# A two-layer hybrid decoder step on one core: GpSimd rounds some weight tiles, the gates become tangents, the convolution starts later, and other keepers

## The reference, cut to what matters

```python
def _mixer(h, st, pos, lb, p):
    ...
    proj = (h @ p['w_in']).astype(f32)
    ...
    conv = xcat[:, :T] * p['gdn_conv_w'][0]
    for j in range(1, GDN_CONV):
        conv = conv + xcat[:, j:j + T] * p['gdn_conv_w'][j]
    conv = jax.nn.silu(conv)
    ...
    gates = jax.nn.sigmoid(proj[..., OFF_GATE:])
    merged = None
    for n, y_b in enumerate((y_rw, y_ret, y_gdn, y_hg)):
        term = gates[..., n * D_MODEL:(n + 1) * D_MODEL] * (y_b @ p['w_branch'][n])
        merged = term if merged is None else merged + term
    out = merged.astype(h.dtype) @ p['w_out']
```

## Time and profile before

| | us |
| --- | --- |
| runs shown | 2711.17, 2693.80, 2695.78 |
| median | 2695.78 |
| profiled execution, its own time | 2704.68 |
| its span in the profile | 2702.9 |
| TensorE busy | 2361.5 (87%) |
| Vector busy | 1138.1 (42%) |
| GpSimd busy | 844.8 (31%) |
| ScalarE busy | 731.2 (27%) |

### The profile page before, as it was taken

How to read it: one execution, slowest core, us unless ns; L and a number is a source line. 1 busy time by engine, 2 the same in 40 slices (tenths; PEclk the granted TensorE clock), 3 DMA queues, 4 the chain that set the end, 5 groups by cost and what they waited for, 6 DMA issues and landing times. The chain is left out here.

```text
span 2702.9 us, 46568 instructions
## 1 busy us (share of the span) xinstructions
PE 2361.5 (87%) x20592; PEld 2176.8 (81%) x20592; DVE 1138.1 (42%) x1558; ACT 731.2 (27%) x915; POOL 844.8 (31%) x602
## 2 busy tenths in 40 slices
PE   5878978689899989999977789777898899999997
PEld 3767866578778979999976679656787699999997
DVE  5164464555444532221233546655734445222212
ACT  2432311322212232222224333104222133322222
POOL 2311210133133434444432213101322234444442
PEclk8988988889999999999988989778999999999998
DMA  6331121111232324322233311111112322222222
GB/s 250 118 110 57 60 72 46 45 51 45 80 102 87 117 88 127 120 91 87 94 120 117 105 54 59 61 55 48 52 52 73 115 77 102 79 94 94 87 93 73
DMA packets 68457, 233.39 MB, mean 86 GB/s; under 512 B 10784, under 2 KB 11296, under 8 KB 67872
## 3 DMA queue, kind: packets, MB, share of 16 engines
q1 hardware_dynamic: 61344, 214.88, 24.1%
q10 hardware_dynamic: 6912, 15.53, 1.6%
HBM read 219.03 MB, written 11.35 MB: 85 GB/s over the span
## 5 line engine op out<-in xcount | busy, mean ns | idle before, releaser
L735 POOL TENSOR_TENSOR ring_lo<-ring,w_hi 128x512 fp32r<-128x512 f32 x552 | 769.9, 1416 | 1429.8 <-ACT w_hi L1355 1361.2
L803 PE MATMUL gm<-H_hi,ring_lo 128*128 128x260 f32 x3456 | 749.2, 299 | 98.1 <-ACT GT L1594 34.1
L803 PE MATMUL gm<-H_hi,w_hi 128*128 128x260 f32 x3456 | 720.9, 290 | 0.0
L803 PE MATMUL gm<-H_lo,w_hi 128*128 128x260 f32 x3456 | 719.9, 291 | 0.0
L803 PEld LDWEIGHTS gm<-H_hi,ring_lo 128*128 128x128 f32 x3456 | 559.6, 197 | 142.5 <-ACT GT L1594 39.9
L803 PEld LDWEIGHTS gm<-H_lo,w_hi 128*128 128x128 f32 x3456 | 554.2, 196 | 2.3 <-issue 1.9
L803 PEld LDWEIGHTS gm<-H_hi,w_hi 128*128 128x128 f32 x3456 | 553.7, 195 | 1.6 <-issue 0.8
L1355 ACT ACTIVATE w_hi<-ring 128x1024 fp32r<-128x1024 f32 x268 | 282.9, 1056 | 447.4 <-PE gm L803 186.0
L752 POOL TENSOR_TENSOR X<-X,GT 128x520 f32<-128x520 f32 x32 | 49.8, 1557 | 323.6 <-DVE GT L2277 323.6
L1279 PE MATMUL gm<-AF_hi,ring_lo 128*128 128x260 f32 x704 | 142.1, 283 | 3.3 <-DVE AF_lo L2301 3.3
L1279 PE MATMUL gm<-AF_hi,w_hi 128*128 128x260 f32 x704 | 141.5, 282 | 0.0
(11 more groups left out here) (410 smaller groups left out, 2750.4 us busy)
## 6 DMA issues: line engine op xcount, KB each, us to landing
ring<-wall SPq DMA_DIRECT2D x372, 512.0 KB, 3.3
WB<-wbranch SPq DMA_DIRECT2D x32, 256.0 KB, 3.6
xsave<-X SPq DMA_DIRECT2D x2, 2080.0 KB, 12.1
X<-xsave ACTq DMA_DIRECT2D x8, 520.0 KB, 5.3
arena<-states ACTq DMA_DIRECT2D x8, 512.0 KB, 3.4
sst<-arena ACTq DMA_DIRECT2D x8, 512.0 KB, 3.7
X<-xt SPq DMA_DIRECT2D x1, 2080.0 KB, 12.1
y<-H SPq DMA_DIRECT2D x4, 520.0 KB, 2.7
```

The source lines that it names most:

```text
L735: pool.tensor_tensor(ring_lo[:, SLOT[i], k], ring[:, SLOT[i], k], hi[:, k].bitcast(F32), ALU.subtract).then_inc(parts_ready, 1)
L803: ins = pe.matmul(out[:, hf, 0:HALF], w[a][:, k, :], src[b][:, k, HALF * hf:HALF * (hf + 1)], start=first and a == "lo", stop=last and a == b)
```

## The change

Six things change:

- **GpSimd's tiles.** A set `BUSY` names stages of mixers; a tile whose rounding by ScalarE would fall behind such a stage is in `held_up` and is rounded by GpSimd. By the plan these are 9 tiles in each layer: gated-delta projections 5 and 7, HG's gate 2, RWKV's gates 2, 5 and 7, retention projections 2 and 5, gated delta's gate 2. GpSimd's roundings go from 8 to 26 in all, ScalarE's from 268 to 250.
- **The convolution** yields twice before its first step, so the first two calls of `beside(2)` do less, and the first evacuation of RWKV's scores comes ahead of it.
- **Gates** are tanh(x/2) in place of the sigmoid; Vector's multiply adds 1 first, and the factor 0.5 goes into the copy that rounds the sum `MG` and the subtraction behind it. ScalarE's table loads go from 74 to 64.
- **Keepers in a modulation bank.** `AT_BANK` puts 18, 18 and 12 keepers ahead of the wait for a bank at a modulation task of HG's stage, at RWKV projection 2 and at gated-delta projection 0. They write to the unused second half of a bank with a modulation product.
- **Other counts of keepers**: `AT_START` 14 to 18; `AT_TILE` as in the diff; 8 ahead of HG's samples; at the norm before the FFN 18 and 26 in place of 22. The two at retention's samples and the argument `busy` in RWKV's scores and inverse go; there the bank was closed, and no instruction changes.
- The order of tasks in the plan, the ring and all transfers stay as they are.

```diff
-AT_START, AT_END, AT_FFN_NORM, AT_INNER = 14, 6, 22, 7
-AT_TILE = {("proj", 2, 2): 20, ("proj", 2, 5): 7, ("proj", 3, 1): 15, ("proj", 3, 6): 8, ("gate", 2, 0): 7}
-AT_SAMPLES = {0: (0, 0), 1: (22, 5), 2: (0, 5), 3: (2, 0)}
+AT_START, AT_END, AT_INNER, AT_SUMS, AT_FFN_NORM = 18, 6, 7, (0, 22), (18, 26)
+AT_TILE = {("proj", 2, 2): 8, ("proj", 3, 6): 5, ("gate", 2, 0): 5, ("gate", 1, 7): 5}
+AT_BANK = {("ada", 0, 18): 18, ("proj", 1, 2): 18, ("proj", 2, 0): 12}
+AT_SAMPLES = {0: (8, 0), 1: (22, 5), 2: (0, 5), 3: (0, 0)}
...
+BUSY = {(RW, 3), (RW, 4), (RW, 6), (GD, 0), (GD, 3), (GD, 5), (GD, len(BEFORE[GD])), (GD, len(BEFORE[GD]) + 6), (RT, 0)}
...
-            on_scalar = {j for j, (i, _) in enumerate(splits)
-                         if j >= mixing + 2 and j - mixing - KT not in (0, 1) or (2 <= j < mixing + 2 and room_after[i] <= at[j - 2])}
+            held_up = {j for j in range(3, mixing + 2)
+                       if any(kind == "mix" and (n, m) in BUSY for kind, n, m in plan[at[j - 3]:at[j - 2]])}
+            on_scalar = {j for j, (i, _) in enumerate(splits) if j not in held_up
+                         and (j >= mixing + 2 and j - mixing - KT not in (0, 1)
+                              or (2 <= j < mixing + 2 and room_after[i] <= at[j - 2]))}
...
                 def begin():
                     kind, n, m = tasks[begun[0]]
+                    if (kind, n, m) in AT_BANK and any(half_only):
+                        keep_busy(AT_BANK[kind, n, m], gm[:, half_only.index(True), 1, HALF:HALF + P128])
                     begun[0] += 1
...
-                        act.activation(h2(GT[:, :]), src, ACT.Sigmoid).then_inc(done, 1)
+                        act.activation(h2(GT[:, :]), src, ACT.Tanh, scale=0.5).then_inc(done, 1)
...
                 def convolution():
 
+                    yield
+                    yield
                     from_scalar()
...
-                    step(tt(MG_lo[:, m, :], MG[:, m, :], MG_hi[:, m, :].bitcast(F32), SUB), x_ready)
+                    step(stt(MG_lo[:, m, :], MG[:, m, :], 0.5, MG_hi[:, m, :].bitcast(F32), MUL, SUB), x_ready)
...
-                            taken(tt(h2(GT[:, :]), src, h2(GT[:, :]), MUL), done)
+                            taken(stt(h2(GT[:, :]), h2(GT[:, :]), 1.0, src, ADD, MUL), done)
```

More of the change, by code:

```diff
@@ L759, in _ @@
                 used = [0, 0]
-                bank_open = [False]
+                bank_open, half_only = [False], [False, False]
                 def keep_busy(n, out=None):
@@ L785, in bank @@
                         pe.wait_ge(evac[g % 2], g // 2)
-                    bank_open[0] = True
+                    bank_open[0], half_only[g % 2] = True, False
                     return gm[:, g % 2]
@@ L847, in ada @@
                     out = bank()
+                    half_only[(used[1] - 1) % 2] = True
                     for k in range(0, KT // 2, 2):
@@ L986, in diagonal_scores, with inverse @@
                     return ins
-                def inverse(cp, busy=0):
+                def inverse(cp):
                     def blocks():
@@ L994, in blocks @@
                                 yield u, u // 2 * NC + 2 * cp + u % 2, slice(a, a + BLK), slice(a + BLK, a + 2 * BLK)
-                    operands(FILL_SHORT, busy=busy)
+                    operands(FILL_SHORT)
                     for u, m, i, j in blocks():
@@ L1144, in rwkv @@
                         yield
-                        operands(busy=4 if cp else 21)
+                        operands()
                         scores(0, cp, pj(RW, 1), WK[:, 0])
@@ L1148, in rwkv @@
                         yield
-                        yield from inverse(cp, 4 if cp else 0)
+                        yield from inverse(cp)
                         for ci in range(2):
@@ L1256, in _ @@
                 coming(-1)
-                if layer + 1 == DEPTH:
-                    keep_busy(AT_FFN_NORM, mx[:, 3, 0:P128])
+                keep_busy(AT_SUMS[layer], mx[:, 3, 0:P128])
                 pe.wait_ge(operands_v, count.next(operands_v))
                 feature_sums()
-                keep_busy(AT_FFN_NORM, mx[:, 3, 0:P128])
+                keep_busy(AT_FFN_NORM[layer], mx[:, 3, 0:P128])
                 for m in range(2 * FT):
@@ L1593, in _ @@
                         gates += 1
-                        act.activation(h2(GT[:, :]), src, ACT.Sigmoid).then_inc(done, 1)
+                        act.activation(h2(GT[:, :]), src, ACT.Tanh, scale=0.5).then_inc(done, 1)
                         g[0] += 1
                         if n == RT and m:
-                            step(act.activation(MG_hi[:, m - 1, :], MG[:, m - 1, :], ACT.Copy), for_vector)
+                            step(act.activation(MG_hi[:, m - 1, :], MG[:, m - 1, :], ACT.Copy, scale=0.5), for_vector)
                     if x in rounds_after and rounds_after[x]:
@@ L1600, in _ @@
                 act.wait_ge(gate_used, gates)
-                step(act.activation(MG_hi[:, KT - 1, :], MG[:, KT - 1, :], ACT.Copy), for_vector)
+                step(act.activation(MG_hi[:, KT - 1, :], MG[:, KT - 1, :], ACT.Copy, scale=0.5), for_vector)
                 for k in range(0, KT, 2):
@@ L2273, in _ @@
                             dve.wait_ge(x_saved, 16)
-                            taken(tt(h2(MG[:, m, :]), src, h2(GT[:, :]), MUL), done)
+                            taken(stt(h2(MG[:, m, :]), h2(GT[:, :]), 1.0, src, ADD, MUL), done)
                             step(dve.tensor_copy(NA[:, :], NA[:, :]), gate_used)
                         else:
-                            taken(tt(h2(GT[:, :]), src, h2(GT[:, :]), MUL), done)
+                            taken(stt(h2(GT[:, :]), h2(GT[:, :]), 1.0, src, ADD, MUL), done)
                             if n == RT:
```

## The result

The changed kernel takes 2686.2 us (median of 8 runs, 2670.4 to 2690.2) against 2702.1 for the kernel before (8 runs, the three shown above among them). The ratio of the two, over all runs, is 0.9932, with a 95% interval from 0.9908 to 0.9956. That is 18.4 us faster (6.5 either way; the two medians are 15.9 apart), where 23.5 were forecast. The profiled execution took 2683.4, 21.3 less than that of before.

A forecast was written before the change was run, and what follows sets the result against it. TensorE was taken to bound the mixing stage, with about 130 us of gaps and slower products after them. Terms 12.6 + 4.8 + 4.0 + 2.0 + 1.8 + 1.3 − 3 = 23.5 off 2695.8 gave 2672.3 us, range 2654 to 2695.

The forecast's parts named there:

- a: RWKV's first scores: evacuating them ahead of Vector's convolution wait gains 6.3 us a layer, 12.6 in all.
- given back: Rival, chance 0.12: Vector meets the convolution's steps later with TensorE behind it, so its gain is 0; 2685 us.
- b: GpSimd rounds nine tiles a layer: gated-delta projection 5 starts without waiting, 2.4 us a layer, 4.8 in all.
- g: GpSimd's eighteen extra roundings slow some Vector operations beside them: 3 us lost, ends 0 and 18.
- c: Keepers ahead of the bank wait at gated-delta projection 0: faster large products, 2.0 us a layer, 4.0 in all.
- d: Keepers ahead of the bank wait at RWKV projection 2: 1.0 us a layer, 2.0 in all.
- e: Eight keepers ahead of HGRN2's samples: layer 1's four products take 1.98 instead of 3.78 us, gaining 1.8.
- f: Gates as tangents: fewer table loads, less one new load and a wider Vector multiply; net gain 1.3 us.
- h: Other keeper changes, including those removed at gated-delta projection 2, stand in waits others end; taken at nothing.
- More than the sum: Rival, chance 0.18: TensorE enters RWKV's inverse at a higher clock, 10 us more gained, 2662.3 us.
- Keepers don't hold the clock: Rival, chance 0.20: the keeper gains at both banks and the samples fall away, 7.8 us; 2680 us.
- Slower: Rival, chance 0.06: GpSimd's rounding delays each of 18 tiles and slows two Vector operations; 48 us more, 2744.

The follow-up runs named there:

- run 2: Changed kernel with ScalarE rounding all 18 tiles again instead of GpSimd: 2686.9 us, ratio to the kernel before 0.9930.
- run 3: Changed kernel with sigmoid gates and Vector's plain multiply again: 2677.4 us, ratio to the kernel before 0.9911.
- run 11: Changed kernel with 20 in place of 8 keepers at gated-delta projection 2: 2672.9 us, ratio to the kernel before 0.9884.
- runs 9 to 12: Changed kernel again, 2684.2 us; with sigmoid gates, 2675.8; with 20 instead of 8 keepers at gated-delta projection 2, 2672.9; with both, 2669.7.
- run 7: Kernel before with all the new tables of keepers and nothing else: ratio to the kernel before 0.9990.
- run 4: Changed kernel with all tables of keepers as before: 2687.1 us, ratio to the kernel before 0.9936.
- run 9: Changed kernel measured and traced once more, nothing altered: 2684.2 us, ratio to the kernel before 0.9922.
- kernels 5 and 8: Kernel before with the later convolution alone, ratio to before 0.9938, and with the tangent gates alone, 0.9965.

## Why the prediction was right or wrong, point by point

The time lay in the range and 5 us from the forecast, within 1% of before, as was likeliest. The terms:

- **a, the convolution: mechanism right, the place measured.** Vector gains 6.3 us from the copy to the second evacuation, as worked out. TensorE gains more, 8.3 and 7.7 by the modulation product behind, since it does not go down in clock (1.16 for the 16 scores instead of 2.08); 3.2 and 2.1 of it (the two traces of the changed kernel) go in the next segment of layer 0, in the first at the clock of 0.66. Alone it brings 16.8 us, undone in the changed kernel 5.7. The forecast's 12.6 lies between. The rival "given back" has a part in it, about 3 us of layer 0 in the trace, but not the whole; how much is lost further on is not shown.
- **b, GpSimd's tiles: right at the place.** Projection 5 starts at its bank's release; without GpSimd it waits 3.47. With the part alone, projections 5 and 6 are 2.1 us shorter in each layer, where the term had 2.4. Over the whole kernel alone and undone differ: alone the part brings 6.5 us, where b and g together had 1.8, and undone in the changed kernel it costs nothing (run 2). At RWKV's gate 7 the forecast said that nothing shows because Vector covers it. GpSimd's timeline there:

```profile
589.90 1.61 POOL L757 TENSOR_TENSOR X<-X,GT 128x520 f32<-128x520 f32 x1 [7.93 <-DVE GT L2287]
591.47 2.21 POOL L737 TENSOR_TENSOR w_hi<-ring,CN 128x1024 fp32r<-128x1024 f32 x1
593.76 2.76 POOL L740 TENSOR_TENSOR ring_lo<-ring,w_hi 128x512 fp32r<-128x512 f32 x2
```

and TensorE's, which answers to the earlier trace rows:

```profile
592.55 1.38 PE L772 MATMUL gm<-CN 128*128 128x128 f32 x10 [0.35 <-ACT GT L1602]
595.35 0.80 PE L808 MATMUL gm<-H_hi,ring_lo 128*128 128x260 f32 x2 [1.41 <-POOL ring_lo L740]
```

  The product ends 4.0 us later than before relative to the gate ahead of it, but by retention projection 1 only 1.0 us is left of it in layer 0 and 1.1 in layer 1. So the cover took three quarters.
- **c: right in layer 0.** 2.5 us for gated-delta 0 and 1, and 3.62 for the thirty steps. In layer 1 the segment is 0 to 1.6 us shorter, and the thirty steps take 5.0 to 5.1 in five of the nine traces with the keepers.
- **d: not in the changed kernel's first trace, but in most of the others.** There the products at RWKV projection 2 are still slow behind the keepers, which leave 3.04 us of the wait bare, and the segment from the modulation product ahead of them to RWKV projection 3 changes by -0.5 and +1.2. In the eight other traces with these keepers that segment takes 23.5 to 23.7 us in fourteen layers of sixteen, and in the five with the old ones 24.6 to 25.4: some 1 us, as forecast. TensorE's timeline in the first trace:

```profile
141.07 0.56 PE L808 MATMUL gm<-H_hi,ring_lo 128*128 128x260 f32 x2 [3.04 <-DVE MT L2230]
141.42 0.64 PE L808 MATMUL gm<-H_lo,w_hi 128*128 128x260 f32 x2
```

- **e: right at the place,** 3.78 to 1.98 in layer 1. Over all traces the first of these products is slow in four layers of ten without the keepers and in none of eighteen with them. Beyond the place no run tells it alone.
- **f: the trace has the signs, the runs don't add up.** The loads went and came where they were said to. RWKV's gates 0 to 6 are 2 us a layer shorter with tangents, where the term had 2.6 (over all traces 0.6 to 4.8 shorter than before with tangents, from 1.9 shorter to 2.0 longer with sigmoids); the load in front of the convolution's sigmoid costs 1.1 to 1.4 by the segment up to it (run 3 against the changed kernel), where the term had 1.3. The tangents alone are 9.5 us faster than before, but in the changed kernel three pairs say 5 to 7 us slower. The term +1.3 lies between; segments whose loads are off the path move by more than the loads do, at one place with the clock (0.66 against 0.83). By the Trainium skill (ScalarE: Activation LUTs, section What ACT_TABLE_LOAD costs) a switch is 2.66 us with its drain. The drain doesn't show here: in the earlier trace rows the gate starts at once behind its load, and in the changed kernel two loads off the path bring some 2 us in a layer, which 1.28 each allow and which is less than one such switch.
- **g: right in size as busy time.** Forecast 3 us; Vector is busy 3.6 us more with the tiles on GpSimd, 0 to 5 over all traces. How much of it is on the path isn't shown. The one case that is shown on the path is not of these tiles: at gated-delta projection 2 it is the low part, which GpSimd makes in all kernels. The operation of the prediction's 1119 ns (L2026) reads one tensor, so it says nothing on operations with two inputs, with which the prediction took it to agree.
- **h: here is the step that failed.** "Those removed at gated-delta projection 2 ... stand in waits that Vector ends", and so were taken at nothing. In the trace they stand behind a wait that ScalarE's evacuation ends, and the product starts when they end, with no further wait. It is the next mixer step that waits for Vector, through ScalarE, and the twelve keepers decide when: without them GpSimd's low part falls on two small operations of Vector, which is 2.0 us later for it, and TensorE comes to the step idle and leaves it slow. By run 11 that costs 1.5 and 1.4 us at the place, and runs 9 to 12 give 8 to 10 us for the whole. At retention projection 1, where thirty instructions went, taking the keepers alone (run 7) changes the time from RWKV's gate 6 to that projection by 0.2 at most, as taken. Together with GpSimd's tiles it is not nothing: that stretch is 0.4 us shorter than before in both layers with the old keepers (run 4), and 1.0 to 1.6 longer in the four traces that have tangents, GpSimd's tiles and the new ones.
- **The rivals.** "More than the sum": the segment behind the scores ran at 0.66, where it was 0.75 before, and took longer; it fell. "Keepers don't hold the clock": false at the places (c in layer 0, d in most traces, e), but the edits' sum comes out as if it were true, since some were put in and others, worth as much, were taken away. "Slower": Vector loses 3.6 us and not 18 times 2.

Two marks of being wrong did show. The waits for GpSimd's low part grew: at RWKV's gate 7 from 0.66 to 1.41, and at retention projection 1, now without keepers, TensorE waits 2.07 us for it in layer 0. And the layers differ by more than 3 us in what they gain, 15.0 in the first and 6.7 in the second by the last product of each. Most of that is RWKV's projections 4 to 7 of layer 0, where the trace of before was slow; in the trace of run 9, the same kernel, the two are 19.2 and 3.9.

So the total of 18.4 is near the forecast in part by luck, by way of errors that cancel. Alone, the convolution, GpSimd's tiles with their contention, and the tangents bring 4.2, 4.7 and 8.2 us more than their terms, and the keepers 5.1 less; together the parts bring 17 us less than the sum of each alone. The keepers cut at gated-delta projection 2 are enough to explain why the new keepers bring so little, 2.7 where the forecast had 7.8. They don't explain the gap of 17 us, since the cut is in the keepers alone as well. That gap, and with it the sign of the tangents in the changed kernel, stays open.

## What to carry to other kernels

A queue's wait should stand behind the work that is ready: two evacuations ahead of a wait for another engine gave TensorE 8.3 and 7.7 us at the place, the largest certain gain here, though not all of it reached the end. Before keepers are cut, look at the next wait as well, and at what moves with the product: here an earlier product brought GpSimd's work onto Vector's path. "Another engine ends this wait" also says nothing of the clock at which the products behind it run. Where a kernel's time follows the clock, test parts both alone and undone, since neither gives the other's number, and read the effect at its place, in several traces: some segments repeat to tenths and others don't.

## What was unexpected of the hardware

A small Vector operation took nearly seven times as long while GpSimd worked, 1.14 us instead of 0.17, and a wait of TensorE hung on it through ScalarE.

Runs of one and the same kernel spread by 11 to 30 us, and the spread goes with the mean granted clock of the run. The changed kernel's fastest run, 2670.4, had a mean clock of 0.939 and its slowest, 2690.2, had 0.929. The four kernels of the last group line up the same way: mean clocks of their runs of 0.933, 0.938, 0.938 and 0.941 beside medians of 2684.2, 2675.8, 2672.9 and 2669.7. Stretches with the same instructions differ by several us along with their clock: RWKV projections 4 to 7 of layer 0 took 72.0 us at a mean of 0.86 in the trace of before, and 65.5 and 65.3 at 0.95 and 0.92 in kernels 5 and 8. So one trace of a kernel can't tell an edit's effect there.
